# Seven-product feed-forward pairs: each product in a bank of its own, or three banks per pair with running sums

## The reference

```
def _swiglu(h, wg, wu, wd):
    return (jax.nn.silu(h @ wg) * (h @ wu)) @ wd
...
    h = _rmsnorm(x, p["norm_ffn1"]) * (1 + sc1) + sh1
    x = x + 0.5 * g1 * _swiglu(h, p["w_ffn1_gate"], p["w_ffn1_up"], p["w_ffn1_down"])
    h = _rmsnorm(x, p["norm_mix"]) * (1 + sc2) + sh2
    m, ckv_n, krope = _mixer(h, p, tables, ctx_ckv, ctx_krope)
    x = x + g2 * m
    h = _rmsnorm(x, p["norm_ffn2"]) * (1 + sc3) + sh3
    x = x + 0.5 * g3 * _swiglu(h, p["w_ffn2_gate"], p["w_ffn2_up"], p["w_ffn2_down"])
```

## Time and profile before

| | |
|---|---|
| median of three runs | 2762.68 us |
| span of the profiled execution | 2759.8 us |
| matmuls on TensorE | 17878 |
| TensorE busy | 2689.4 us, 97% of the span |
| VectorE busy | 2017.3 us, 73% |
| ScalarE busy | 1216.1 us, 44% |
| GpSimd busy | 622.6 us, 23% |

### The profile page before, as it was taken

How to read it: one execution, slowest core, us unless ns; L and a number is a source line. 1 busy time by engine, 2 the same in 40 slices (tenths; PEclk the granted TensorE clock), 3 DMA queues, 4 the chain that set the end, 5 groups by cost and what they waited for, 6 DMA issues and landing times. The chain is left out here.

```text
span 2759.8 us, 44748 instructions
## 1 busy us (share of the span) xinstructions
PE 2689.4 (97%) x17878; PEld 2536.0 (92%) x17878; DVE 2017.3 (73%) x2736; ACT 1216.1 (44%) x1998; POOL 622.6 (23%) x323
## 2 busy tenths in 40 slices
PE   6999999999999999999999999999999999999997
PEld 3999999977799999999989999999778999999997
DVE  6878878766534788887888879787664358776876
ACT  5533435556422543343564335355563236443433
POOL 1322422022100124232321413210220002242230
PEclk9999999999999999999999999999999999999999
DMA  6445432210121253423224444322101222212312
GB/s 239 152 147 161 146 123 68 72 56 26 43 84 63 92 168 116 130 99 109 93 101 152 139 159 145 102 75 67 46 27 64 74 65 85 92 63 84 105 49 77
DMA packets 86446, 273.02 MB, mean 99 GB/s; under 512 B 8736, under 2 KB 10016, under 8 KB 86112
## 3 DMA queue, kind: packets, MB, share of 16 engines
q1 hardware_dynamic: 84800, 265.60, 29.1%
q10 hardware_dynamic: 1440, 4.56, 0.5%
HBM read 267.21 MB, written 2.92 MB: 98 GB/s over the span
## 5 line engine op out<-in xcount | busy, mean ns | idle before, releaser
L624 POOL TENSOR_TENSOR sums_raw<-raw_pairs 128x1024 f32<-128x1024 f32 x88 | 238.3, 2708 | 1627.9 <-DVE weights_lo L1706 1050.2
L652 PE MATMUL ps<-h_hi,weights_hi 128*128 128x322 f32 (+1 forms) x1408 | 440.3, 313 | 8.6 <-DVE t_lo L1706 3.1
L656 PE MATMUL ps<-h_hi,weights_lo 128*128 128x322 f32 (+1 forms) x1408 | 437.4, 311 | 0.0
L654 PE MATMUL ps<-h_lo,weights_hi 128*128 128x322 f32 (+1 forms) x1408 | 436.8, 310 | 0.0
L1706 DVE TENSOR_TENSOR weights_lo<-sums_raw,weights_hi 128x1024 fp32r<-128x1024 f32 (+2 forms) x296 | 329.7, 1114 | 56.5 <-ACT weights_hi L1237 26.7
L652 PE MATMUL ps<-t_hi,weights_hi 128*128 128x322 f32 (+1 forms) x1056 | 332.2, 315 | 5.3 <-DVE h_lo L1706 5.3
L652 PE MATMUL ps<-a_hi,weights_hi 128*128 128x320 f32 x1408 | 325.1, 312 | 3.3 <-DVE tmp L1884 2.5
L656 PE MATMUL ps<-t_hi,weights_lo 128*128 128x322 f32 (+1 forms) x1056 | 327.5, 310 | 0.0
L654 PE MATMUL ps<-t_lo,weights_hi 128*128 128x322 f32 (+1 forms) x1056 | 326.4, 309 | 0.0
L654 PE MATMUL ps<-a_lo,weights_hi 128*128 128x320 f32 x1408 | 321.5, 309 | 0.0
L656 PE MATMUL ps<-a_hi,weights_lo 128*128 128x320 f32 x1408 | 321.5, 309 | 0.0
(11 more groups left out here) (273 smaller groups left out, 5680.6 us busy)
## 6 DMA issues: line engine op xcount, KB each, us to landing
raw_pairs<-in_w_up SPq DMA_DIRECT2D x87, 1024.0 KB, 4.9
wm<-in_w_mod SPq DMA_DIRECT2D x88, 512.0 KB, 3.9
raw<-in_w_merge SPq DMA_DIRECT2D x32, 704.0 KB, 4.0
sums_raw<-in_w_down SPq DMA_DIRECT2D x56, 384.0 KB, 3.2
wm<-in_w_mod SPq DMA_DIRECT2D x80, 256.0 KB, 3.0
sums_raw<-in_w_down SPq DMA_DIRECT2D x64, 320.0 KB, 3.0
raw<-in_w_in SPq DMA_DIRECT2D x16, 512.0 KB, 3.6
raw<-in_w_out SPq DMA_DIRECT2D x16, 512.0 KB, 3.5
```

The source lines that it names most:

```text
L624: nc.gpsimd.tensor_tensor(sums_raw[:, UNIT:3 * UNIT].rearrange("p (s c) -> p s c", s=2), w.rearrange("p (s c) -> p s c", s=2)[:, :, 0:UNIT ...
L652: nc.tensor.matmul(out, whi, v, start=first, stop=False)
L654: nc.tensor.matmul(out, whi, v, start=False, stop=False)
L656: mm = nc.tensor.matmul(out, wlo, v, start=False, stop=last)
```

## The change

The first pair of a chunk (`lone`) keeps the old scheme, with its banks given by name. In every other pair (72 of 88) the seven products share three banks. P1 and then P2 go into one bank, the second onto the first. ScalarE copies P1 into a second bank before P2 starts; there P6 is accumulated onto it, then P7, then P4. P5 has the third bank, and P3 is accumulated onto it. Two new ScalarE copies, `copy_u2` and `copy_u3`, take P1+P6 and P1+P6+P7 (320 columns) into SBUF before the next product goes onto the bank. `c12` and `c22` add these copies to the bank of P5 and P3. TensorE gets waits for them: P2 for `copy_a1`, P7 for `copy_u2`, P4 for `copy_u3`, P3 for `c22`. On VectorE `u2`, `u2_p5` and `u3` go; `c11` and `c21` multiply with `r_one` as they read PSUM, and the two scalings handle only the first half. The down tiles use the bank pairs in another rotation, and the first waits for `c11` instead of `c22` and `c21`.

```
+    if lone(pair):
+        return FIRST_BANKS[name]
+    ...
+    return {"P1": 0, "P2": 0, "P5": 2, "P3": 2, "P6": 4, "P7": 4, "P4": 4}[name] + other
...
     def p3():
         pe.wait_ge(s_lo34, g + 1)
+        if not lone(g):
+            pe.wait_ge(s_c22, g + 1)
...
     pe.wait_ge(s_lo34, g + 1)
+    if lone(g):
+        pe.wait_ge(s_a1, g + 1)
+    else:
+        pe.wait_ge(s_u2c, joint_count(g))
     up_product(g, "P7", HALF, unit(6), first_half(h_hi, 0), first_half(h_lo, 0))
     if following:
         p1(g + 1)
...
     pe.wait_ge(s_lo22, g + 1)
+    if lone(g):
+        pe.wait_ge(s_usum, lone_count(g) * 3 - 2)
+    else:
+        pe.wait_ge(s_u3c, joint_count(g))
     up_product(g, "P4", ext, unit(2), differences(t_hi, TB, TW), differences(t_lo, TB, TW))
...
             if j == 0:
-                pe.wait_ge(s_c22, last + 1)
-                pe.wait_ge(s_c21, last + 1)
+                pe.wait_ge(s_c11, last + 1)
...
+            def copy_u2(g):
+                act.wait_ge(s_product, DONE[g, "P6"])
+                act.wait_ge(s_c12, g)
+                nc.scalar.activation(u2_copy, bank(up_bank(g, "P6"), 0, HALF), ACT.Copy).then_inc(s_u2c, 1)
+
+            def copy_u3(g):
+                act.wait_ge(s_product, DONE[g, "P7"])
+                act.wait_ge(s_c22, g)
+                nc.scalar.activation(u3_copy, bank(up_bank(g, "P7"), 0, HALF), ACT.Copy).then_inc(s_u3c, 1)
...
                     if not first:
+                        copy_u2(g)
                         a_part(g - 1)
                     if last:
                         hi_down(step, c, 0)
+                        copy_u3(g)
```

More of the change, by code:

```diff
@@ L177, with lone, lone_count, joint_count @@
 DONE = product_counts()
-NAMES = {n: of for of, n in DONE.items()}
-UP_BANKS = 6
-def up_bank(pair, name):
-    f, t = divmod(pair, PAIRS)
-    first = f * PAIRS + FIRSTS[f][chunk_of(pair)[0]]
-    return (DONE[pair, name] - DONE[first, "P1"]) % UP_BANKS
+FIRST_BANKS = {"P1": 0, "P2": 5, "P3": 3, "P4": 4, "P5": 2, "P6": 4, "P7": 0}
+def lone(pair):
+    return chunk_of(pair)[1]
+def lone_count(pair):
+    return pair // PAIRS * 4 + chunk_of(pair)[0] + 1
+def joint_count(pair):
+    return pair + 1 - lone_count(pair)
+def up_bank(pair, name):
+    if lone(pair):
+        return FIRST_BANKS[name]
+    f = pair // PAIRS
+    other = (pair % PAIRS - FIRSTS[f][chunk_of(pair)[0]]) % 2
+    return {"P1": 0, "P2": 0, "P5": 2, "P3": 2, "P6": 4, "P7": 4, "P4": 4}[name] + other
 def mod_pieces(vector):
@@ L647, in _, with product @@
                 pe.sem_inc(started, START)
-            def product(outs, whi, wlo, xhi, xlo, first, last):
+            def product(outs, whi, wlo, xhi, xlo, first, last, onto=False):
                 for n, (out, v) in enumerate(zip(outs, xhi)):
-                    nc.tensor.matmul(out, whi, v, start=first, stop=False)
+                    nc.tensor.matmul(out, whi, v, start=first and not onto, stop=False, skip_group_check=onto)
                 for out, v in zip(outs, xlo):
-                    nc.tensor.matmul(out, whi, v, start=False, stop=False)
+                    nc.tensor.matmul(out, whi, v, start=False, stop=False, skip_group_check=onto)
                 for out, v in zip(outs, xhi):
-                    mm = nc.tensor.matmul(out, wlo, v, start=False, stop=last)
+                    mm = nc.tensor.matmul(out, wlo, v, start=False, stop=last, skip_group_check=onto)
                 return mm
@@ L770, in up_product @@
             def up_product(g, name, cols, weights, xhi, xlo, before=None):
[L772 to L777, removed]
+                b, onto = up_bank(g, name), not lone(g) and name not in ("P1", "P5")
                 for i, (whi, wlo) in enumerate(weights):
@@ L803, in p1 @@
                         pe.wait_ge(s_xupd, xupd0 + KT * c - 1)
+                    elif not lone(g - 1):
+                        if lone(g - 2):
+                            pe.wait_ge(s_usum, lone_count(g - 2) * 3)
+                        else:
+                            pe.wait_ge(s_c11, g - 1)
                     up_product(g, "P1", ext, unit(0), second_half(h_hi, 0), second_half(h_lo, 0))
@@ L853, in part @@
                     def part(j, ks):
-                        out = halves(pair((j + 1) % 3))
+                        out = halves(pair(j % 3))
                         w = down_slot(j, n)
@@ L1360, in cycle @@
                     else:
+                        if not first:
+                            copy_u3(g)
                         hi_s(g + 1)
@@ L1931, in cycle @@
                     c11(g)
-                    u2(g)
+                    if first:
+                        u2(g)
                     if following:
                         lo_12(g + 1)
-                    u2_p5(g)
+                    if first:
+                        u2_p5(g)
                     if g == g0:
@@ L1938, in cycle @@
                         inverse_columns(nn, step)
-                    if not first:
+                    if first:
+                        u3(g)
+                        c22(g)
+                    else:
                         a_rest(g - 1)
-                    u3(g)
-                    c22(g)
+                        c22(g)
+                        up_scaled(g)
                     if last:
@@ L1947, in cycle @@
                     c21(g)
-                    up_scaled(g)
+                    if first:
+                        up_scaled(g)
                     if last:
```

88 lines of the change are left out of this document (66 added, 22 removed).

## The result

| | before | after |
|---|---|---|
| median (4 runs each) | 2762.65 us (2762.57 to 2762.83) | 2777.26 us (2772.34 to 2777.58) |
| span of the profiled execution | 2759.8 us | 2775.6 us (its own time 2777.41) |

The ratio is 1.0047, interval 1.0035 to 1.0059: the change made the kernel slower by about 13 us. The forecast was 2771.3 us. The direction is as forecast; the size is not, and the median lies 0.3 us over the upper end of the range. The spans differ by 15.8 us, where the sum said 8.6. About 1.1 us of that is chance: in every run whose own time and span are both known (after: 2777.41 and 2775.6) the time lies 1.8 to 2.1 us over the span, so the profiled execution before took about 2761.6 us, 1.1 under its median. The 2.9 us between span and median, given ahead of the prediction as what lies around the first and the last instruction, hold that chance too.

The account below looks back on a forecast made before the run. TensorE, busy 2689.4 of 2759.8 us, bounds the kernel, VectorE nearly as full. Chunk ends 11.7 plus second pairs 4.8 less gains 7.9 gave +8.6 us: span 2768.4, median 2771.3 us; own range 2767 to 2776, 8-in-10 range 2762.5 to 2777.

Parts of the forecast that it names:

- its two causes: Copies without cover at the 16 chunk ends, 11.7 us, and in the second pair of each step, 4.8 us.
- The handoff at a chunk's end: P4 waits for copy_u3 right behind P7: 0.77 us at 13 ends, 0.55 at three, 11.7 us in all.
- The second pairs: In each step's second pair P7 waits for copy_u2 behind hi_12: 0.94 us in three steps, 2.0 in the fourth.
- The middle of a chunk: Copies between products inside a chunk are all hidden; if copy_u2 were not, 72 pairs would pay.
- The gains: Fourth step's first chunk 2.6, c21 waits 2.8, lower clock behind one 1.5, a_lo waits 1.0: 7.9 us.
- So the weights land ahead of P7's end everywhere, and I add nothing.: At chunk ends, hi_down's DMA comes earlier with lo_22, so copy_u3 behind hi_down waits no longer: 0 us.
- The bound of 7 us: At chunk ends, if the down weights' DMA keeps its time: up to 7 us, about 2776; rival's chance 0.11.
- The lower level behind the 2 us wait of the fourth step: Clock rival: the second pair's 2.0 us wait is followed by the lower clock, +1.5 us, 2773; even chance.
- the granted clock falls at new places: One of three signs, beside P7 waiting mid-chunk and free chunk ends, that the forecast is wrong; no size given.
- a half-width one should take about the 0.48 us of a narrow addition: VectorE's two scalings per pair: 0.35 us less each; with three additions 2.1 us per pair, about 150 us busy.
- The rule on cycling banks: Skill's rule that brief pauses between matmul groups can make the clock swing; the trace was taken to speak against it.
- Its rival: Every new wait of TensorE is followed by the lower clock: 20 x 1.5 = +30 us, 2801; chance 0.03.

Follow-up runs that it names:

- both: The changed kernel with the last pair ordered P6, P2, P7, P5, P4, P3, copies ahead, and the second pair's copy_u2 on VectorE: 2759.56 us, again 2758.04 us.
- the first and the second experiment: The changed kernel with copy_u3 ahead of hi_down: 2775.49 us; that with the last pair also ordered P6, P2, P7, P5, P4, P3: 2763.00 us.

## Why the prediction was right, and where it was not

**The sign and its two causes are right.** The handoff at a chunk's end was forecast at 0.77 us, and moving one product between removes it. That the size fits so well is in part luck. The 0.77 held 0.10 for the late second matmul and 0.06 for the way from ScalarE to TensorE. In the trace after, 0.77 to 0.79 us (13 of 16 ends) lie between the two starts alone, because that way takes 0.14 us and the copy 0.44; the second matmul adds 0.07. About 0.03 of it is made up again, and the offset stays 0.82 us higher per end. The second pairs: 1.0 us for the three (0.94 forecast), 2.0 for the fourth (2.0). The waits stand where they were foreseen, 16 and 4, with 0.62 us idle instead of 0.5.

**The middle of a chunk is right.** The copies there cost nothing, and 0.33 us more for each cost nothing either.

**The gains are right in kind and near in size:** -9.1 us in the profiles against -7.9; and half of the scalings alone, without a copy, gave -6.4. But 1.5 of both sums is the lower clock behind 1357 us, seen in one execution of the kernel before. As the rows below show, a wait of that length isn't followed by it each time, so 7.6 is the safer figure for what the runs gave.

**The step that failed first:** "So the weights land ahead of P7's end everywhere, and I add nothing." The step let the DMA move with `lo_22`, and gave it the duration of one trace. In front of the down weights goes a load of 1 MB. For the second chunk's end, the DMA view gives its size, and the time from issue to landing in us: in the kernel before (227 to 241 us), then after (228 to 243), then with `copy_u3` ahead of `hi_down` (228 to 243), then the two measurements of "both" (226 to 241).

```profile
raw_pairs<-in_w_up SPq DMA_DIRECT2D x1, 1024.0 KB, 5.1
```

```profile
raw_pairs<-in_w_up SPq DMA_DIRECT2D x1, 1024.0 KB, 7.5
```

```profile
raw_pairs<-in_w_up SPq DMA_DIRECT2D x1, 1024.0 KB, 5.1
```

```profile
raw_pairs<-in_w_up SPq DMA_DIRECT2D x1, 1024.0 KB, 7.5
```

```profile
raw_pairs<-in_w_up SPq DMA_DIRECT2D x1, 1024.0 KB, 5.2
```

VectorE did get to `lo_22` earlier. After, the load was issued at 232.75 instead of 231.31, while the products around it had moved by 2.1 us, so 0.7 us earlier against these; and it followed four loads of the modulation weights after 3.75 instead of 4.41 us. One could think that it ran into these. But with `copy_u3` ahead of `hi_down` it was issued at 232.66, with the same 3.75 us behind the same four loads, and was not late; and "both" is one kernel, issued its load at 230.81 and at 230.79, and had 7.5 us once and 5.2 once. So the duration differs between executions of the same order. In the eight profiles of kernels with the shared banks, the load at the second chunk's end of the first and of the third step took 7.2 to 7.9 us ten times and 4.8 to 5.2 six times; in the kernel before it took 5.1 both times. That the closer issue makes the long duration likelier is possible and not shown. What failed is the overlap with a margin of nothing: `hi_down` ended just as P7 was done, and the step added nothing for a load that takes 2.4 us longer. The bound of 7 us was there. It cost 1.5 us once in this profile, and up to three ends were late in others.

**The clock was only half in the sum.** The lower level behind the 2 us wait of the fourth step was given an even chance; the one behind the late end, and the longer stretch in the first mixer, were not in it. That "the granted clock falls at new places" was one of the forecast's own signs of being wrong, and in this profile it did. In the mixer (windows of 575 to 605 us) the granted clock was 0.89, where the kernel before had 0.94 in 565 to 595. No wait for a feed-forward copy lies near. How much of this is the change's? For the mixer, the two profiles of "both" tell, from 576 to 590 us:

```profile
576.00:590.00 14.00, 12.89 (x51) 10.03 (x52) 10.54 (x14) 6.12 (x8) 0.00 (x0) 0.76 0.30 85
```

```profile
576.00:590.00 14.00, 12.29 (x60) 9.65 (x61) 13.04 (x17) 6.54 (x9) 0.00 (x0) 1.00 0.26 85
```

It is the same kernel, once at a granted clock of 0.76 and once at 1.00, and 2.5 of the 3.2 us between the two spans arise in this stretch. So the 2.8 us of the first mixer need not be the change's. For the two waits, the clock of other kernels at these places tells. From the kernel with each copy twice: P4 at the second chunk's end, P7 in the fourth step's second pair, and the windows around the two (the granted clock is the number behind the brackets of POOL).

```profile
243.61 0.38 PE L668 MATMUL ps<-t_hi,weights_hi 128*128 128x322 f32 x1 [2.44 <-ACT tmp L1370]
...
2346.33 0.38 PE L668 MATMUL ps<-h_hi,weights_hi 128*128 128x320 f32 x1 [2.31 <-ACT tmp L1364]
...
241.00:247.00 6.00, 3.56 (x25) 3.42 (x24) 2.71 (x5) 2.67 (x6) 0.00 (x0) 1.00 0.13 29
...
2340.00:2355.00 15.00, 12.69 (x87) 12.45 (x86) 12.67 (x17) 11.07 (x20) 5.73 (x3) 1.00 0.21 72
```

Longer waits than those of the trace after were followed by the full clock here, at both places. So were the waits of 1.82 and 1.98 us at the same places in the kernel with the old waits at the first tile (granted clock 1.00 from 241 to 247 and from 2340 to 2355). Nor did the clock fall (1.00 around it) behind the wait of 1.99 us in the fourth step in the first and the second experiment. So the 3.0 us behind the two waits belong to that execution and not to every one. The kernel with the old waits at the first tile has neither, and reached the same span (2775.7 us): against the trace after it lost 1.2 us at a chunk end that was late and 2.8 us in the second mixer. And one of the four runs of the changed kernel took 2777.11 us at a mean granted clock of 0.995, where the profiled one had 0.990. What the median contains of the clock stays open. The runs of one kernel spread by 5 us (the kernel before from 2761.19 to 2766.34), and the 0.3 us by which the median lies over the range is far inside that. By size, the medians differ by 14.6 us and the ratio gives 9.7 to 16.3; the handoffs, the second pairs and the gains add up to 12.3 + 5.0 - 9.1 = 8.2, or 9.7 with a gain of 7.6, and late weights add 1.5 where they come. That is the lower end of what the ratio gives, and the rest is not settled.

**VectorE's busy time fell by 65.5 us, not 150.** The step "a half-width one should take about the 0.48 us of a narrow addition" was wrong for one of the two. `a_lo` became dearer too, though it didn't change: 1267 ns in the mean before, 1527 after. The two half scalings after (columns: busy us, mean ns, idle time before):

```profile
L1963 DVE TENSOR_TENSOR tmp<-tmp,r_one 128x320 f32<-128x320 f32 x72 | 59.3, 824 | 2.5
...
L1981 DVE TENSOR_TENSOR tmp<-tmp,r_one 128x320 f32<-128x320 f32 x72 | 35.5, 493 | 7.5
```

The two half scalings have the same form, and one takes 824 ns and the other 493. The last section shows why. No wait of TensorE came of it in the list above: the waits for `c21` and `a_lo` are gone all the same.

**The rule on cycling banks.** Its rival had 0.03 and was rightly put low: behind the waits of 0.62 us the granted clock is 1.00 (the window from 128 us above). The Trainium skill (TensorE: Matmul & The Clock Gate, "A second HAM failure mode: psum-queue depth-cycling") describes swings between the levels from short pauses between groups of matmuls; with one short pause per chunk no run here shows that.

## What to carry to other kernels

When products are made to share a bank, look at each place where the product between two uses of it is missing (the last pair, the first one): there the copy has no cover, and it cost about 0.8 us at each ordinary chunk end here; put another product between. A load's time from issue to landing can differ by over 40% between executions of the same kernel (5.2 and 7.5 us here), so an instruction that waits for one has to be priced by its margin and by several executions, and a wait that vanishes in one profile is no proof of the edit. And busy time taken off an engine is not what its removed rows add up to: here the rows left behind moved up into GpSimd's instructions and waited them out, and under half of the sum arrived.

## What the hardware showed that was not expected

**VectorE beside GpSimd.** In the middle of a chunk, first GpSimd and VectorE before, then after:

```profile
437.29 2.83 POOL L624 TENSOR_TENSOR sums_raw<-raw_pairs 128x1024 f32<-128x1024 f32 x1 [6.36 <-DVE weights_lo L1706]
```

```profile
438.80 1.87 DVE L1706 TENSOR_TENSOR weights_lo<-raw_pairs,weights_hi 128x512 fp32r<-128x512 f32 x1
```

```profile
430.62 2.83 POOL L640 TENSOR_TENSOR sums_raw<-raw_pairs 128x1024 f32<-128x1024 f32 x1 [10.47 <-DVE weights_lo L1763]
433.53 1.62 POOL L644 TENSOR_TENSOR sums_raw<-sums_raw,raw_pairs 128x512 f32<-128x512 f32 x1
435.22 1.75 POOL L647 TENSOR_TENSOR sums_raw<-sums_raw,raw_pairs 128x512 f32<-128x512 f32 x1
```

```profile
431.29 0.49 DVE L1919 TENSOR_TENSOR tmp<-ps,r_one 128x322 f32<-128x322 f32 x1
431.70 2.29 DVE L1763 TENSOR_TENSOR weights_lo<-raw_pairs,weights_hi 128x512 fp32r<-128x512 f32 x1
433.92 1.91 DVE L1763 TENSOR_TENSOR a_lo<-tmp,a_hi 128x640 fp32r<-128x640 f32 x1
...
436.39 0.94 DVE L1963 TENSOR_TENSOR tmp<-tmp,r_one 128x320 f32<-128x320 f32 x1
...
438.79 0.68 DVE L1763 TENSOR_TENSOR weights_lo<-raw_pairs,weights_hi 128x512 fp32r<-128x512 f32 x1
```

While GpSimd works (430.62 to 436.97), operations with both inputs in SBUF are stretched: 2.29 us for what takes 0.68 us at 438.79, 0.94 for what takes 0.49. Those that read one input from PSUM keep their 0.49 us. The ends tell more than the durations. GpSimd's first instruction ends at 433.45, and the rounding inside it at 433.99, 0.54 us later. The second ends at 435.15, and `a_lo` at 435.83, 0.68 later. The third ends at 436.97, and the half scaling at 437.33, 0.36 later. Each of these is the operation's own time (0.68, 0.82, 0.49) less 0.13 or 0.14. Before, it is the same: GpSimd's first ends at 440.12, and the rounding at 440.67, 0.55 later, though it lasted 1.87 us and not 2.29. `a_lo` ended 0.68 us after GpSimd's instruction at all 57 places of either trace where it began inside one. So such an operation makes no headway until GpSimd's instruction is over, and its row counts the wait as busy.

That is where the relief went. In the timeline of the kernel before, `u2`, `u2_p5` and `u3` lay in GpSimd's time (0.48 us each, at 438.40, 440.59 and 442.42, with GpSimd at work from 437.29 to 443.65) and cost no more than elsewhere. Without them the rounding and `a_lo` start earlier in GpSimd's instructions and end no earlier against them: 1.87 and 1.50 us before, 2.29 and 1.91 after. With 0.45 for the half scaling, which now lies there, and less 0.18 for `lo_s`, which no longer does (1.39 before, 1.21 after), that is 1.1 of the 2.1 us per pair.

**The clock behind a wait.** Waits of 1.88 and 1.99 us for a copy were followed by the lower level in one profile. Waits of 1.68 to 2.44 us for a copy were not in five others, eight of them, at the same or like places of nearly the same program. A wait of that length is a risk of 1.5 us, not a price.

**A copy out of PSUM.** Its row lasts 0.42 to 0.44 us, the second of two adds 0.33, and TensorE starts 0.14 us after its end (0.06 was taken).
